# A 1408-column gate/up unit cut into three matmul pieces of 470, 470 and 468 columns in place of four of 352

## The chip, the cores and the metric

The program runs on one core of a Trainium2 chip, as one launch. The metric is device microseconds of that core for one execution; lower is better. Engines are named as in the profile: PE is TensorE (PEld its weight loads), DVE is VectorE, ACT is ScalarE, POOL is GpSimd, SP is SyncE, which starts the weight transfers. PSUM is the memory that TensorE writes: eight banks, each 512 float32 values wide in every one of 128 partitions.

## The reference: what is computed

Two decoder layers on 512 prompt tokens and 64 sample tokens, 576 rows of 1024 values. Each layer has three mixers (gated linear attention, a gated recurrence, dilated window attention), an output projection and a channel mixer. The channel mixer of layer 0 is a dense SwiGLU; that of layer 1, which the change touches, is a mixture of 8 experts of width 1408, two for each row:

```python
def swiglu(h, w_gate, w_up, w_down):
    return (jax.nn.silu(h @ w_gate) * (h @ w_up)) @ w_down

def moe_swiglu(h, w_router, w_gate, w_up, w_down):
    logits = (h @ w_router).astype(jnp.float32)
    top_v, top_i = lax.top_k(logits, TOP_K)
    gates = jax.nn.softmax(top_v, axis=-1)
    combine_w = jnp.sum(jax.nn.one_hot(top_i, N_EXPERTS, dtype=jnp.float32) * gates[..., None], axis=-2)
    out = jnp.zeros(h.shape, jnp.float32)
    for e in range(N_EXPERTS):
        out = out + combine_w[..., e:e + 1] * swiglu(h, w_gate[e], w_up[e], w_down[e]).astype(jnp.float32)
    return out.astype(h.dtype)
```

## The kernel before

**Items.** Rows are gathered by expert into items of 160 rows at most: 128 rows ("many") and 32 more ("few"). The count of items is data dependent; in the profiled run there are eight. Item 0 is written out (`item(None)`), the others run in a loop whose body is the same code. An expert's hidden width of 1408 is worked in two halves of `HID` = 704, and `CH` = 352 is half of that.

**Units.** Weights come in units of 128 input rows. A gate/up unit is 1408 columns wide: 704 columns of the gate, then the 704 of the up product for the same half. One half takes `KC` = 8 such units, since the model width is 8 x 128. A down unit is 1024 columns wide; a half has 6 or 5 of them. An item's order on TensorE, in `item`: 8 gate/up units of half 0, then 5 down units left over from the item before, then 8 gate/up units of half 1, then the 6 down units of half 0.

**Three passes.** Each float32 operand is split into a rounded part (hi) and the remainder (lo). ScalarE rounds a unit (L1087), VectorE takes the remainder (L2106), and `many_rows` (L1599 to L1606) multiplies every piece of the unit three times: hi by hi, hi by lo, lo by hi. The 128 rows stand still in the array and the weights stream past, so a piece of 352 columns is a matmul of 128x352. Three buffers (`NW` = 3) hold split units, so ScalarE starts on unit j + 3 once TensorE has finished unit j.

**Banks.** `gate_up` writes the unit's four pieces into banks 0 to 3 from column 0: the gate is in banks 0 and 1, the up product in banks 2 and 3. The 32 few rows use bank 4 (`few_rows`, L1608), with unsplit weights, after the units k = 1 and k = 5. Down units write banks 5 and 6.

**The end of a half.** When the eighth unit is done, ScalarE takes silu of the gate (`gates`, L1111 and L1112 for the many rows, L1113 for the few) and counts `silu_ready` (named gates_ready in the program) up by one after each. VectorE multiplies by the up product (`hidden`, L2113 and L2115 for the many rows, L2117 and L2118 for the few), and the last product counts `hid_ready`. Before its first product VectorE waits for the first silu, before its second for the second, before the third for the third. TensorE meanwhile runs two down units and then waits for `hid_ready` in `turn_hidden`, which transposes the hidden rows (L1633, L1636). In half 0 of item 0 there are no down units, so the wait comes at once.

What sets the order is the program text alone: each engine runs its own list in order, with semaphores between the lists.

Of the kernel before, what the change touches and what calls it, by code (L numbers as in the profile page):

```python
# [23 lines left out]
ALU = mybir.AluOpType  # L24
ACT = mybir.ActivationFunctionType
AX = mybir.AxisListType

P = 128
# [4 lines left out]
KC = D_MODEL // P  # L33
# [7 lines left out]
FE = 11  # L41
# [57 lines left out]

CH = FE * P // 4  # L100
HID = 2 * CH
TURNED = (range(0, HID // P), range(HID // P, FE))
U_FIRST = 2 * KC + len(TURNED[0])
U_BODY = 2 * KC + FE
# [101 lines left out]
def build(nc, d):  # L206

    ctx = ExitStack()
    with ctx:
# [6 lines left out]
        def tiles(ap, n):  # L216
            return ap.rearrange("p (n t) -> p n t", n=n)
# [27 lines left out]
        with ExitStack() as over:  # L245
# [4 lines left out]
            Xh, Xl = (tiles(over.enter_context(nc.sbuf_tensor(n, [P, KC * P], F32R)), KC) for n in ("item_in_hi", "item_in_lo"))  # L250

        V = tiles(sb("values", (TT + 1) * D_MODEL), TT + 1)
        LIN = sb("linear", N_LIN)
# [12 lines left out]
        def carve(base, *sizes):  # L266
            out, o = [], 0
            for s in sizes:
                out.append(base[:, o:o + s])
                o += s  # L270
            return out
# [66 lines left out]
        ht_few = tiles(qk_[:, 64 + 2 * FE * P:64 + 2 * FE * P + FE * CAP2], FE)  # L338
        FEW_AT = 2 * P
        hid_rows = [LIN[0:w, n * FE * P:(n + 1) * FE * P] for n, w in enumerate((P, CAP - P))]  # L340
        gate_a, gate_b, gate_few = carve(LIN[:, 2 * FE * P:2 * FE * P + 3 * CH], CH, CH, CH)

        X_tok = tiles(LIN[:, 0:(TT + 1) * D_MODEL], TT + 1)
        XT = [H_tok[:, st, :] for st in range(2)]
# [23 lines left out]
        ps = ctx.enter_context(nc.psum_tensor("ps", [P, 8, 512], F32))  # L368
# [4 lines left out]
        def split(ap):  # L373
# [49 lines left out]
        silu_ready, hid_ready, ht_ps, ht_hi, ht_ready = (sem(n) for n in (  # L423
            "gates_ready", "hidden_rows_ready", "hidden_in_psum", "hidden_rounded", "hidden_split"))
# [405 lines left out]
        def _(act):  # L830
# [23 lines left out]
            for L in range(DEPTH):  # L854
# [138 lines left out]
                for n in range(N_STEP + 3):  # L993
# [7 lines left out]
                    k = n - 2  # L1001
# [6 lines left out]
                    k = n - 3  # L1008
# [57 lines left out]
            for tt in range(TT + 1):  # L1066
                rows = P if tt < TT else NS
                act.wait_ge(xtok_ps, tt + 1)
                k = 2 + 2 * (tt % 3)
# [3 lines left out]
            for tt in range(TT + 1):  # L1073
                rows = P if tt < TT else NS
                act.wait_ge(htok_ps, tt + 1)
                k = 2 * (tt % 2)
# [31 lines left out]
            def gates(before, j):  # L1108

                act.wait_ge(unit_done, item_unit(before, j) + (UD_ITEMS + 1))  # L1110
                nc.scalar.activation(gate_a, ps[:, 0, 0:CH], ACT.Silu).then_inc(silu_ready, 1)  # L1111
                nc.scalar.activation(gate_b, ps[:, 1, 0:CH], ACT.Silu).then_inc(silu_ready, 1)  # L1112
                nc.scalar.activation(gate_few[0:DH], ps[0:DH, 4, 0:CH], ACT.Silu).then_inc(silu_ready, 1)  # L1113

            def copy_hidden(step, half):
# [41 lines left out]
        def _(pe):  # L1157
# [33 lines left out]
            for L in range(DEPTH):  # L1191
# [6 lines left out]
                for half in range(2):  # L1198
                    for u in range(4):
                        w = split_unit(ring_n, 2)  # L1200
                        ring_n += 1
                        for kk in range(2):
                            k = 2 * u + kk
# [61 lines left out]
                for ct in range(CT):  # L1265
# [53 lines left out]
                    o = ATS_AT[ct]  # L1319
# [76 lines left out]
                for n in range(N_STEP + 3):  # L1396
                    if n < N_STEP:
# [4 lines left out]
                        for c in range(0, w, 256):  # L1402
                            e = min(c + 256, w)
# [5 lines left out]
                    k = n - 3  # L1409
                    if 0 <= k < N_STEP:  # L1410
# [4 lines left out]
                        for kb in range(i + 1):  # L1415
                            for h in range(2):
                                o, f = slice(h * DH, h * DH + DH), 512 + (2 * hp + h) * DH
# [3 lines left out]
                    k = n - 2  # L1421
# [16 lines left out]
                for b in range(NB + 2):  # L1438
# [12 lines left out]
                    if b < NB:  # L1451
# [4 lines left out]
                        for a in range(2):  # L1456
                            for hp in range(4):
                                o = slice(32 * hp, 32 * hp + 32)
                                nc.tensor.matmul(ps[o, a, :], Qs[:, b, hp, :], kc[hp // 2][:, hp % 2, a * 512:a * 512 + 512], start=True, stop=True)
                        for hp in range(4):  # L1460
                            o = slice(32 * hp, 32 * hp + 32)
                            op = nc.tensor.matmul(ps[o, 2, 0:NS], Qs[:, b, hp, :], QK[:, 4 + hp, SEQ:T], start=True, stop=True)
                        op.then_inc(ssc_done, 1)
                    if 1 <= b <= NB:
# [6 lines left out]
                        for half in range(2):  # L1471
                            vc = tiles(piece_landed(pe, L, b - 1, 2 + half), 4)
                            for c in range(4):
                                for m in range(2):
                                    r, e = slice(64 * m, 64 * m + 64), slice(256 * m, 256 * m + 256)
                                    op = nc.tensor.matmul(out[r, e], pt[:, 4 * half + c, r], vc[:, c, e], start=(half, c) == (0, 0), stop=False)  # L1476
                            if half:
                                for m in range(2):
                                    r, e = slice(64 * m, 64 * m + 64), slice(256 * m, 256 * m + 256)
# [119 lines left out]
            def many_rows(before, j, x, outs, first, last):  # L1599

                pe.wait_ge(ew_split, item_unit(before, j) + 1)
                w = [t[:, j % NW, :] for t in (EWh, EWl)]
                for o, out in outs:
                    for n, (a, b) in enumerate(PASSES):
                        op = nc.tensor.matmul(out, x[a], w[b][:, o:o + out.shape[-1]], start=first and n == 0, stop=last and n == 2)  # L1605
                op.then_inc(unit_done, 1)  # L1606
# [7 lines left out]

            def gate_up(before, j0):
                for k in range(KC):
                    many_rows(before, j0 + k, [x[:, k, :] for x in (Xh, Xl)], [(c * CH, ps[:, c, 0:CH]) for c in range(4)], k == 0, k == KC - 1)
                    if k % 4 == 1:
                        for k2 in range(k - 1, k + 3):
                            few_rows(before, j0 + k2, x_few[:, k2, :], ps[:, 4, 0:CH], k2 == 0, k2 == KC - 1)  # L1620
# [63 lines left out]
        def _(dve):  # L1684
            v = nc.vector
# [34 lines left out]
            for L in range(DEPTH):  # L1720
# [138 lines left out]
                for ct in range(CT):  # L1859
# [6 lines left out]
                    o = ATS_AT[ct]  # L1866
# [51 lines left out]
                for n in range(N_STEP + 1):  # L1918
# [11 lines left out]
                    k = n - 1  # L1930
# [8 lines left out]
                for b in range(NB + 2):  # L1939
# [22 lines left out]
                    if b >= 2:  # L1962
                        dve.wait_ge(os_turned, NB * L + b - 1)
                        o = ps[:, 6 + b % 2, 0:P].rearrange("p (h q) -> p h q", h=4)
# [143 lines left out]
            def hidden(step, half):  # L2108

                o = half * HID  # L2110
                few = hid_rows[1]
                dve.wait_ge(silu_ready, step * 3 + 1)
                v.tensor_tensor(hid_rows[0][:, o:o + CH], ps[:, 2, 0:CH], gate_a, ALU.mult)  # L2113
                dve.wait_ge(silu_ready, step * 3 + 2)
                v.tensor_tensor(hid_rows[0][:, o + CH:o + HID], ps[:, 3, 0:CH], gate_b, ALU.mult)  # L2115
                dve.wait_ge(silu_ready, step * 3 + 3)
                v.tensor_tensor(few[:, o:o + CH], ps[64:96, 4, 0:CH], gate_few[0:32], ALU.mult)  # L2117
                v.tensor_tensor(few[:, o + CH:o + HID], ps[96:128, 4, 0:CH], gate_few[32:64], ALU.mult).then_inc(hid_ready, 1)  # L2118

# [135 lines left out]
```

## Time and profile before

| what | value |
|---|---|
| timed runs | 2201.57, 2205.87, 2208.22 us |
| their median | 2205.87 us |
| span of the profiled execution (first to last instruction) | 2200.3 us |
| mean granted TensorE clock over it | 0.965 |
| gate/up matmuls of the many rows | 3 x 512 of 128x352 |
| experts' stage in the span | about 1638 to 2185 us |

For the profiled execution the page gives no time beside its span of 2200.3 us; what stands before the first and behind the last instruction is not in it. Each row of a timeline gives a start and a duration. Matmuls overlap and their ends are modelled, so what a matmul costs the engine is read from start to start, not from its duration. A bracket at a row's end says how long the engine was idle before it and which instruction ended that wait.

### The profile page before, as it was taken

The numbers are of one execution on the slowest core, as the hardware profiler recorded it, in microseconds if no ns is written. First come the engines' busy times: TensorE is split into PE (matmuls) and PEld (weight loads), VectorE is DVE, ScalarE is ACT, GpSimd is POOL, SyncE is SP. The second block draws the span as 40 slices with busy tenths as digits, with TensorE's granted clock in tenths as the row PEclk, the third lists the DMA queues.
The fourth block names the chain that finished last, engine by engine and source line by source line (L and its number), as shares of the span: only waits on it lengthen the run. The fifth ranks groups of instructions, "written<-read, shape, count | busy, mean of one in ns | idle before, by whom it ended". The sixth has DMA issues, their size and how long they took to land. (4 is left out here: it accounts for less than half of the span.)

```text
span 2200.3 us, 36316 instructions
## 1 busy us (share of the span) xinstructions
PE 2020.9 (92%) x15091; PEld 1726.2 (78%) x15091; DVE 1011.8 (46%) x1365; ACT 870.0 (40%) x1208; POOL 273.7 (12%) x330
## 2 busy tenths in 40 slices
PE   7999787789999999999999788788978999999997
PEld 5999676546899999998899777546777777777775
DVE  3235655551333322323134564542126666676664
ACT  3356333420222212223247333521225565666664
POOL 2000643000100000002000552000040110111001
PEclk9999889999999999999999978999989999999998
DMA  4452103293375347421452201284335877787874
GB/s 176 158 186 78 71 1 133 81 403 113 115 286 173 123 178 257 152 76 45 153 192 85 106 1 58 118 356 155 109 137 209 285 269 278 273 287 259 285 286 119
DMA packets 78408, 375.46 MB, mean 171 GB/s; under 512 B 10160, under 2 KB 10576, under 8 KB 69424
## 3 DMA queue, kind: packets, MB, share of 16 engines
q1 hardware_dynamic: 70992, 354.47, 43.9%
q0 software_dynamic: 7296, 19.23, 3.0%
q8 instruction: 95, 1.56, 0.3%
q14 instruction: 25, 0.20, 0.0%
HBM read 357.21 MB, written 84.37 MB: 201 GB/s over the span
## 5 line engine op out<-in xcount | busy, mean ns | idle before, releaser
L2106 DVE TENSOR_TENSOR expert_weights_lo<-weight_ring,expert_weights_hi 128x1408 fp32r<-128x1408 f32 (+1 forms) x141 | 203.4, 1475 | 100.6 <-ACT expert_weights_hi L1087 100.1
L1087 ACT ACTIVATE expert_weights_hi<-weight_ring 128x1408 fp32r<-128x1408 f32 (+1 forms) x144 | 178.3, 1263 | 97.9 <-PE ps L1605 97.9
L1167 PE MATMUL ps<-ffn_in_hi,weights_hi 128*128 128x288 f32 x704 | 208.7, 296 | 5.8 <-DVE weights_lo L1983 3.3
L1167 PE MATMUL ps<-ffn_in_lo,weights_hi 128*128 128x288 f32 x704 | 207.7, 295 | 0.0
L1167 PE MATMUL ps<-ffn_in_hi,weights_lo 128*128 128x288 f32 x704 | 207.0, 294 | 0.0
L1167 PE MATMUL ps<-proj_in_hi,proj_weights_hi 128*128 128x288 f32 x608 | 183.5, 302 | 0.0
L1605 PE MATMUL ps<-expert_weights_hi,item_in_hi 128*128 128x352 f32 x512 | 172.1, 336 | 9.2 <-DVE expert_weights_lo L2106 5.6
L1167 PE MATMUL ps<-proj_in_lo,proj_weights_hi 128*128 128x288 f32 x608 | 179.3, 295 | 0.0
L1167 PE MATMUL ps<-proj_in_hi,proj_weights_lo 128*128 128x288 f32 x608 | 178.7, 294 | 0.0
L1605 PE MATMUL ps<-expert_weights_hi,item_in_lo 128*128 128x352 f32 x512 | 166.2, 325 | 0.0
L1605 PE MATMUL ps<-expert_weights_lo,item_in_hi 128*128 128x352 f32 x512 | 166.0, 324 | 0.0
L1183 PE MATMUL ps<-constants 128*128 128x128 f32 x1004 | 142.4, 295 | 21.0 <-DMA normed_or_mixed<-s_hgrn 16.8
L1183 PEld LDWEIGHTS ps<-constants 128*128 128x128 f32 x1004 | 130.0, 206 | 28.4 <-issue 18.9
L2106 DVE TENSOR_TENSOR expert_weights_lo<-residual,expert_weights_hi 128x1408 fp32r<-128x1408 f32 (+1 forms) x72 | 103.5, 1442 | 80.0 <-ACT expert_weights_hi L1087 80.0
L1167 PEld LDWEIGHTS ps<-ffn_in_hi,weights_hi 128*128 128x128 f32 x704 | 131.9, 187 | 6.4 <-DVE weights_lo L1983 3.8
L1167 PEld LDWEIGHTS ps<-ffn_in_hi,weights_lo 128*128 128x128 f32 x704 | 132.6, 188 | 0.0
L1167 PEld LDWEIGHTS ps<-ffn_in_lo,weights_hi 128*128 128x128 f32 x704 | 132.2, 188 | 0.0
L1983 DVE TENSOR_TENSOR weights_lo<-weight_ring,weights_hi 128x1024 fp32r<-128x1024 f32 (+1 forms) x60 | 79.7, 1332 | 112.8 <-ACT weights_hi L1037 112.8
L1087 ACT ACTIVATE expert_weights_hi<-residual 128x1408 fp32r<-128x1408 f32 (+1 forms) x72 | 88.9, 1235 | 102.9 <-PE ps L1605 102.9
L1161 PE MATMUL ps<-normed_or_mixed,weight_ring 128*128 128x288 f32 x512 | 126.4, 410 | 1.1 <-DVE normed_or_mixed L1967 1.1
L1605 PEld LDWEIGHTS ps<-expert_weights_hi,item_in_hi 128*128 128x128 f32 x512 | 97.5, 191 | 33.7 <-DVE expert_weights_lo L2106 20.1
L1161 PEld LDWEIGHTS ps<-normed_or_mixed,weight_ring 128*128 128x128 f32 x512 | 98.2, 192 | 28.7 <-DVE normed_or_mixed L1967 1.5
(342 smaller groups left out, 4296.6 us busy)
## 6 DMA issues: line engine op xcount, KB each, us to landing
weight_ring<-w_gu_moe SPq DMA_DIRECT2D x89, 704.0 KB, 6.4
ok_s<-kcache SPq DMA_DIRECT2D x16, 2032.0 KB, 10.3
ov_s<-vcache SPq DMA_DIRECT2D x16, 2032.0 KB, 9.3
weight_ring<-w_dn_moe SPq DMA_DIRECT2D x55, 512.0 KB, 5.8
residual<-w_gu_moe SPq DMA_DIRECT2D x39, 704.0 KB, 6.4
weight_ring<-w_gu SPq DMA_DIRECT2D x44, 512.0 KB, 3.6
scratch<-kcache SPq DMA_DIRECT2D x20, 1024.0 KB, 10.6
scratch<-vcache SPq DMA_DIRECT2D x20, 1024.0 KB, 12.2
```

What stands on the lines that cost most here:

```text
L1087: nc.scalar.activation(EWh[:, j % NW, 0:w], slot[:, 0:w], ACT.Copy).then_inc(ew_hi, 1)
L1161: op = nc.tensor.matmul(out_pair[:, a, :], w, rhs[:, a * HALF:a * HALF + HALF], start=k == 0, stop=k == kn - 1)
L1167: op = nc.tensor.matmul(out, x, y, start=k == 0 and n == 0, stop=k == kn - 1 and n == 2)
L1183: nc.tensor.matmul(ps[:, bank, col:col + P], const["ones"], const["ones"], start=True, stop=True, skip_group_check=True)
L1605: op = nc.tensor.matmul(out, x[a], w[b][:, o:o + out.shape[-1]], start=first and n == 0, stop=last and n == 2)
L1983: v.tensor_tensor(Wl[:, j % NSPLIT, 0:w], ring[:, n % R, 0:w], Wh[:, j % NSPLIT, 0:w], ALU.subtract).then_inc(w_split, 1)
L2106: v.tensor_tensor(EWl[:, j % NW, 0:w], slots[q][:, 0:w], EWh[:, j % NW, 0:w], ALU.subtract).then_inc(ew_split, 1)
```

## The change

A gate/up unit's 1408 columns are cut at 470 and 940 in place of 352, 704 and 1056. Three pieces lie in banks 0, 1 and 2. The gate then ends in the middle of the second piece: its columns 470 to 703 are in bank 1 at 0 to 233, and the first 236 columns of the up product follow them in the same bank, at 234 to 469. ScalarE's two silus are 470 and 234 columns wide, VectorE's two products 236 and 468. VectorE waits for both silus before its first product.

```diff
+CUTS = (0, 470, 940, 2 * HID)
...
-        gate_a, gate_b, gate_few = carve(LIN[:, 2 * FE * P:2 * FE * P + 3 * CH], CH, CH, CH)
+        gate_many, gate_few = carve(LIN[:, 2 * FE * P:2 * FE * P + 3 * CH], 2 * CH, CH)
...
                 act.wait_ge(unit_done, item_unit(before, j) + (UD_ITEMS + 1))
-                nc.scalar.activation(gate_a, ps[:, 0, 0:CH], ACT.Silu).then_inc(silu_ready, 1)
-                nc.scalar.activation(gate_b, ps[:, 1, 0:CH], ACT.Silu).then_inc(silu_ready, 1)
+                nc.scalar.activation(gate_many[:, 0:CUTS[1]], ps[:, 0, 0:CUTS[1]], ACT.Silu).then_inc(silu_ready, 1)
+                nc.scalar.activation(gate_many[:, CUTS[1]:HID], ps[:, 1, 0:HID - CUTS[1]], ACT.Silu).then_inc(silu_ready, 1)
                 nc.scalar.activation(gate_few[0:DH], ps[0:DH, 4, 0:CH], ACT.Silu).then_inc(silu_ready, 1)
...
-                    many_rows(before, j0 + k, [x[:, k, :] for x in (Xh, Xl)], [(c * CH, ps[:, c, 0:CH]) for c in range(4)], k == 0, k == KC - 1)
+                    many_rows(before, j0 + k, [x[:, k, :] for x in (Xh, Xl)], [(o, ps[:, c, 0:e - o]) for c, (o, e) in enumerate(zip(CUTS, CUTS[1:]))], k == 0, k == KC - 1)
...
-                dve.wait_ge(silu_ready, step * 3 + 1)
-                v.tensor_tensor(hid_rows[0][:, o:o + CH], ps[:, 2, 0:CH], gate_a, ALU.mult)
                 dve.wait_ge(silu_ready, step * 3 + 2)
-                v.tensor_tensor(hid_rows[0][:, o + CH:o + HID], ps[:, 3, 0:CH], gate_b, ALU.mult)
+                up1 = CUTS[2] - HID
+                v.tensor_tensor(hid_rows[0][:, o:o + up1], ps[:, 1, HID - CUTS[1]:CUTS[2] - CUTS[1]], gate_many[:, 0:up1], ALU.mult)
+                v.tensor_tensor(hid_rows[0][:, o + up1:o + HID], ps[:, 2, 0:2 * HID - CUTS[2]], gate_many[:, up1:HID], ALU.mult)
                 dve.wait_ge(silu_ready, step * 3 + 3)
```

One line is added near the top, so most line numbers are higher by one after the change; the products of `hidden` are then L2115, L2116, L2118 and L2119.

On TensorE, the second gate/up unit of item 0 stands so before (expert_weights are the unit's hi and lo parts, item_in the item's 128 rows):

```order
L1605 MATMUL ps<-expert_weights_hi,item_in_hi 128x352
L1605 MATMUL ps<-expert_weights_lo,item_in_hi 128x352
L1605 MATMUL ps<-expert_weights_hi,item_in_lo 128x352
L1605 MATMUL ps<-expert_weights_hi,item_in_hi 128x352
L1605 MATMUL ps<-expert_weights_lo,item_in_hi 128x352
L1605 MATMUL ps<-expert_weights_hi,item_in_lo 128x352
L1605 MATMUL ps<-expert_weights_hi,item_in_hi 128x352
L1605 MATMUL ps<-expert_weights_lo,item_in_hi 128x352
L1605 MATMUL ps<-expert_weights_hi,item_in_lo 128x352
L1605 MATMUL ps<-expert_weights_hi,item_in_hi 128x352
L1605 MATMUL ps<-expert_weights_lo,item_in_hi 128x352
L1605 MATMUL ps<-expert_weights_hi,item_in_lo 128x352
```

and so after the change:

```order
L1606 MATMUL ps<-expert_weights_hi,item_in_hi 128x470
L1606 MATMUL ps<-expert_weights_lo,item_in_hi 128x470
L1606 MATMUL ps<-expert_weights_hi,item_in_lo 128x470
L1606 MATMUL ps<-expert_weights_hi,item_in_hi 128x470
L1606 MATMUL ps<-expert_weights_lo,item_in_hi 128x470
L1606 MATMUL ps<-expert_weights_hi,item_in_lo 128x470
L1606 MATMUL ps<-expert_weights_hi,item_in_hi 128x468
L1606 MATMUL ps<-expert_weights_lo,item_in_hi 128x468
L1606 MATMUL ps<-expert_weights_hi,item_in_lo 128x468
```

Twelve matmuls became nine; nothing changed places with anything else, and all other units of item 0 and of the loop's body change in the same way.

On VectorE, at the end of half 0 of item 0 (linear holds the gates and the hidden rows), before:

```order
L2113 TENSOR_TENSOR linear<-ps,linear 128x352 [waits gates_ready]
L2115 TENSOR_TENSOR linear<-ps,linear 128x352 [waits gates_ready]
L2117 TENSOR_TENSOR linear<-ps,linear 32x352 [waits gates_ready]
L2118 TENSOR_TENSOR linear<-ps,linear 32x352
L2106 TENSOR_TENSOR expert_weights_lo<-weight_ring,expert_weights_hi 128x1408 [waits expert_unit_hi]
```

and after:

```order
L2115 TENSOR_TENSOR linear<-ps,linear 128x236 [waits gates_ready]
L2116 TENSOR_TENSOR linear<-ps,linear 128x468
L2118 TENSOR_TENSOR linear<-ps,linear 32x352 [waits gates_ready]
L2119 TENSOR_TENSOR linear<-ps,linear 32x352
L2107 TENSOR_TENSOR expert_weights_lo<-weight_ring,expert_weights_hi 128x1408 [waits expert_unit_hi]
```

Two products over 128 partitions are still two; the first is narrower, the second wider, and the wait between them now stands, with the later count, ahead of the first.

On ScalarE, at the same place, before:

```order
L1111 ACT_TABLE_LOAD
L1111 ACTIVATE linear<-ps 128x352 [waits unit_done]
L1112 ACTIVATE linear<-ps 128x352
L1113 ACTIVATE linear<-ps 64x352
L1087 ACTIVATE expert_weights_hi<-weight_ring 128x1408 [waits unit_done,expert_unit_in7]
```

and after:

```order
L1112 ACT_TABLE_LOAD
L1112 ACTIVATE linear<-ps 128x470 [waits unit_done]
L1113 ACTIVATE linear<-ps 128x234
L1114 ACTIVATE linear<-ps 64x352
L1088 ACTIVATE expert_weights_hi<-weight_ring 128x1408 [waits unit_done,expert_unit_in7]
```

The first silu is wider and the second narrower by as much; the order is the same.

## Rows read from the trace of the kernel before

**Rows 1.** The page: span, TensorE's busy line, the chain by line.

```profile
span 2200.3 us, 36316 instructions
PE 2020.9 (92%) x15091; PEld 1726.2 (78%) x15091; DVE 1011.8 (46%) x1365; ACT 870.0 (40%) x1208; POOL 273.7 (12%) x330
PE ps L1605 16%; PE ps L1612 5%; PE ps L1161 4%; DVE expert_weights_lo L2106 1%; ACT expert_weights_hi L1087 1%; POOL slot_table L780 1%; DMA scratch<-vcache 1%; PE ps L1633 1%; PE ps L1592 0%; PE ps L1636 0%; PE ps L1594 0%; PE ps L1476 0%; PE ps L1564 0%; DMA values<-normed_rows,attn_qk 0%; DMA slot_table<-attn_qk 0%
```

**Rows 2.** Busy by stretch; columns: stretch, length, busy (count) by engine, PEclk, DMA.

```profile
1638.00:1690.00 52.00, 46.72 (x327) 39.02 (x328) 25.48 (x22) 23.38 (x22) 2.92 (x8) 0.90 0.51 187
1757.00:1824.00 67.00, 66.22 (x513) 52.22 (x512) 45.70 (x41) 41.08 (x48) 8.43 (x10) 1.00 0.79 277
```

**Rows 3.** Waits of TensorE, 1638 to 2200; columns: us in total, times, longest.

```profile
PE ps L1605 <- DVE expert_weights_lo L2106: 6.0, 15, 0.5
PE ps L1633 <- DVE linear L2118: 3.4, 1, 3.4
```

**Rows 4.** Line L1605: ns min/median/max, first and last start, forms.

```profile
L1605 PE MATMUL ps<-expert_weights_hi,item_in_hi x512: 320/322/662, 1638.2 to 2160.7; 128*128 128x352 f32 x171
```

**Rows 5.** Timeline, TensorE, gate/up units; columns: start us, us, what.

```profile
1779.16 0.32 PE L1605 MATMUL ps<-expert_weights_hi,item_in_hi 128*128 128x352 f32 x1
1782.97 0.32 PE L1605 MATMUL ps<-expert_weights_hi,item_in_hi 128*128 128x352 f32 x1
...
1676.39 0.32 PE L1605 MATMUL ps<-expert_weights_lo,item_in_hi 128*128 128x352 f32 x1
1683.76 0.32 PE L1605 MATMUL ps<-expert_weights_hi,item_in_lo 128*128 128x352 f32 x1
```

**Rows 6.** Timeline, TensorE: 288 and 512 columns elsewhere, 512 in down units.

```profile
45.27 0.39 PE L1213 MATMUL ps<-proj_weights_hi,proj_in_hi 128*128 128x512 f32 x1
50.71 0.39 PE L1213 MATMUL ps<-proj_weights_hi,proj_in_hi 128*128 128x512 f32 x1
...
1099.79 0.29 PE L1167 MATMUL ps<-proj_in_hi,proj_weights_lo 128*128 128x288 f32 x1
1102.99 0.29 PE L1167 MATMUL ps<-proj_in_hi,proj_weights_lo 128*128 128x288 f32 x1
...
1798.35 0.39 PE L1605 MATMUL ps<-expert_weights_lo,hidden_turned_hi 128*128 128x512 f32 x1
1803.40 0.40 PE L1605 MATMUL ps<-expert_weights_hi,hidden_turned_lo 128*128 128x512 f32 x1
```

**Rows 7.** Timeline, TensorE, at the lower clock.

```profile
1667.90 0.49 PE L1605 MATMUL ps<-expert_weights_hi,item_in_lo 128*128 128x352 f32 x1
1669.95 0.49 PE L1605 MATMUL ps<-expert_weights_hi,item_in_hi 128*128 128x352 f32 x1
```

**Rows 8.** Timeline, all engines, where the gates are taken.

```profile
1824.80 0.32 PE L1605 MATMUL ps<-expert_weights_hi,item_in_lo 128*128 128x352 f32 x1
1825.16 0.46 ACT L1111 ACTIVATE linear<-ps 128x352 f32<-128x352 f32 x1 [0.84 <-PE ps L1605]
1825.52 0.46 ACT L1112 ACTIVATE linear<-ps 128x352 f32<-128x352 f32 x1
1825.65 0.52 DVE L2113 TENSOR_TENSOR linear<-ps,linear 128x352 f32<-128x352 f32 x1
1827.16 0.52 DVE L2118 TENSOR_TENSOR linear<-ps,linear 32x352 f32<-32x352 f32 x1
1827.48 0.39 PE L1605 MATMUL ps<-expert_weights_hi,hidden_turned_lo 128*128 128x512 f32 x1
1827.71 1.23 DVE L2106 TENSOR_TENSOR expert_weights_lo<-weight_ring,expert_weights_hi 128x1024 fp32r<-128x1024 f32 x1
...
1827.73 0.64 PEld L1633 LDWEIGHTS ps<-constants,linear 128*128 128x128 f32 x6 [0.29 <-DVE linear L2118]
...
1832.95 0.50 PE L1605 MATMUL ps<-expert_weights_hi,hidden_turned_hi 128*128 128x512 f32 x1
```

**Rows 9.** Line L2118: who waited for it; columns: us, times.

```profile
  PEld ps L1633: 8.0, 16
```

## The prediction, made before the changed kernel ran

> **What bounds the kernel now.** I read the page first: TensorE is busy for 92% of the span, and of the lines on the chain that ended last, L1605 has the largest share, 16% [rows 1]. L1605 is the line of the change. Next comes the table by stretch: in the experts' stage, over 67 us of one item, TensorE is busy for 66.22 us at a granted clock of 1.00, that is the 2.4 GHz level, while VectorE has 45.70 us and ScalarE 41.08 us [rows 2]. So the stage is TensorE's own stream, and a microsecond taken from it or put into it shows in the end. The waits say where the stream is broken. From 1638 us on, TensorE waits 15 times for a split unit (6.0 us in all), which is the start of a run of gate/up units after down units, and once for 3.4 us at L1633, the transposes of the hidden rows [rows 3]. That last row hides something: TensorE's weight loader waits at the same line for VectorE's last product L2118, 16 times out of 16 [rows 9]. So the end of each half is a tie between two engines, and the change touches both sides of it. These are the two terms: the cost of a gate/up unit, and the time of `hid_ready`.
>
> **Term 1: nine matmuls in place of twelve.** A half has 8 units, an item 2 halves, and there were 8 items: 128 units, 12 matmuls each, 1536 in all; the row has one pass of three, 512 [rows 4]. The columns stay 3 x 1408 = 4224 a unit, so a gain can only come from what a matmul costs beside its columns. I read that from start to start. Elsewhere in the program, two streams with the same kind of 128x128 weights run without a break: 24 steps of 512 columns take 50.71 - 45.27 = 5.44 us, 226.7 ns each; 24 steps of 288 columns take 1102.99 - 1099.79 = 3.20 us, 133.3 ns each [rows 6]. The line through both has 0.4167 ns a column (one column per cycle at 2.4 GHz) and 13.3 ns beside. For 352 it gives 160.0 ns. The units themselves: two units from 1779.16 to 1782.97 are 24 steps of 158.8 ns, and 46 steps from 1676.39 to 1683.76 are 160.2 ns [rows 5]. The line holds to 1%.
>
> So 470 columns should take 209.2 ns and 468 take 208.3: a unit is 6 x 209.2 + 3 x 208.3 = 1880 ns. Before it is 12 x 158.8 = 1905 or 12 x 160.2 = 1922. The gain is 25 to 42 ns a unit; I take 34. At the 1.2 GHz level it is nothing: 7 steps from 1667.90 to 1669.95 take 293 ns each, which is 352 columns at one per cycle with nothing beside [rows 7]. Some two or three units at the start of the stage run there, so 125 units count: 125 x 34 ns = 4.2 us less.
>
> The bounds. Above, 42 x 125 = 5.3 us. Below, the down units of the same stage take 229.5 ns for 512 columns (22 steps from 1798.35 to 1803.40), not 226.7 [rows 6]. If a wide matmul in this stage has that supplement, 470 lies between 160.2 at 352 and 229.5 at 512, at 211.3 ns, and a unit at 1899: 6 to 23 ns a unit, down to 0.8 us. I stay at 4.2, as the nearest rows, those of the same units, are on the clean line.
>
> Here a rule of the Trainium skill can be set against the rows. "TensorE: Matmul & The Clock Gate", section "Back-to-back issue gap", gives a step of N/2.4 + 2.5 ns. Three steps fewer would then be worth 7.5 ns a unit, an estimate of 1 us in all. The rows have 13.3 at two widths, so the measurement decides.
>
> **What hides behind a unit.** ScalarE and VectorE split units at widths that don't change, and TensorE's unit gets shorter by 2%. Within a run of gate/up units TensorE shows no wait before (24 steps of equal length across unit limits) [rows 5]. The first unit after down units still starts when its split is ready; that chain begins at a down unit and isn't touched, so those 6.0 us stay [rows 3].
>
> **Term 2: the hidden rows come later.** The timeline at the end of a half reads so [rows 8]. The unit's last matmul starts at 1824.80. ScalarE's first silu runs 1825.16 to 1825.62, the second 1825.52 to 1825.98. VectorE's first product starts at 1825.65, 0.03 us behind the first silu. Four products later L2118 ends at 1827.16 + 0.52 = 1827.68, and the transposes' weight load starts at 1827.73, 0.05 us after it. TensorE had its last down matmul at 1827.48 and would have gone on one 512 step later, at about 1827.71. The tie is won by VectorE by about 0.02 us.
>
> After the change VectorE's first product waits for both silus. The two silus have 704 columns in two instructions, as before, so the second ends as before at 1825.98 and the product starts at 1826.01: 0.36 us later. The two products have 704 columns in two instructions, as before, and the two of the few rows don't change; all four run back to back for the same 2.03 us. So `hid_ready` comes 0.36 us later, and as TensorE already waits for it, the whole of it is on TensorE. That happens 16 times: 16 x 0.36 = 5.8 us more.
>
> The bounds: four products of 0.52 us, the length of L2113 and L2118, would be 2.08 us end to end, and they take 2.03. If that overlap of 0.05 us is lost or doubled with the new widths, the delay is 0.41 or 0.31 us: 5.0 to 6.6 us in all. What is queued behind the waiting product on VectorE are the remainders of the next units: L2106 at 1827.71 goes to 1828.07. The down unit that follows the transposes starts at 1832.95, and moves with them [rows 8]; 3.6 us of cover stay. ScalarE's roundings behind the silus are not moved. DMA is at a share of 0.79 and sees the same units at the same pace [rows 2].
>
> **The sum.** -4.2 + 5.8 = +1.6 us. The profiled span is 2200.3 us, and the timed median 2205.87 stands 0.25% over it; the terms are microseconds of the same stage, so I add them to the median: 2207.5 us. By the bounds of this case alone it is -5.3 + 5.0 = -0.3 at best and -0.8 + 6.6 = +5.8 at worst, 2205.6 to 2211.7. A difference under 0.3%, 6.6 us, can't be told from no change by a measurement of this kernel.
>
> **Rivals.**
>
> *The gain without the wait.* The transposes don't come later, because TensorE's down units stretch or VectorE catches up. Then only term 1 is left: 2205.9 - 4.2 to - 5.3, about 2201. Against it stands the wait at 16 places of 16 [rows 9]: there is no slack on VectorE's side. For it, only that the tie is close. Chance 0.07. It too is under 6.6 us.
>
> *The new starts cost (slower).* Before, each piece of a unit starts at a multiple of 1408 bytes in the weights' row; after, two of the three start at 1880 and 3760 bytes. No row shows a stream from such a place. If TensorE reads those slower, the price falls on 6 matmuls of 9, 768 in all. From 6.6 ns a matmul, 3% of 209, it adds 5.1 us to the 1.6 and the kernel is slower than can be missed: at 5%, 10 ns, +9.6 us, 2215. For it: nothing but that the place is new. Against it: a unit's pieces start at four different places before, and their mean step is on the line [rows 5, 6]. Chance 0.08.
>
> *A matmul costs by the piece, not by the column (faster).* A unit would fall to 9/12 of 1.91 us, 0.48 us less, 60 us over 125 units: 2152 with term 2. The same section of the Trainium skill gives 131 ns for 512 columns and 81 for 128 as the sustained pace of load and matmul pairs, a far weaker growth with the width than one column per cycle; an estimate from it would be 24 us less. The rows have 133.3 ns at 288 and 226.7 at 512 [rows 6], so the chance is 0.01.
>
> **How the numbers follow.** The forecast has 0.84 (nearly all of it within 0.3%), the gain alone 0.07 (within 0.3%), new starts 0.08 (slower), cost by the piece 0.01 (faster). Scatter of the timed runs, 2201.57 to 2208.22, can push either way by a few microseconds, which I count as 0.03 more for each side. So faster 0.04, within 0.3% 0.85, slower 0.11. The range runs from the gain alone to just over the upper bound of the forecast: 2201 to 2212.5.
>
> **What would show it.** Term 1: steps of 209 ns at the 470 columns, 128 units of 1.88 us; 211 or more says that the supplement of the down units is in it, 216 or more the new starts. Term 2: VectorE's first product starting 0.03 us behind the second silu, and 0.6 us from the start of the last down matmul to the transposes' weight load, where it was 1827.73 - 1827.48 = 0.25. The weight loader's waits at that line grow from 8.0 us by 5.8. The forecast is wrong if the whole stage moves by more than 7 us, or if it gets shorter by over 1 us.

## The result and the profile after

The changed kernel is slower: 2211.73 us median against 2202.53 for the kernel before, 22 runs each, ratio 1.0036 with a 95% interval of 1.0026 to 1.0047. That is +7.9 us (5.7 to 10.4), by the mean times; the medians are 9.2 us apart. The time lies in the stated range and on the side of the forecast's sign, but the forecast was +1.6 us and "within 0.3%" had 0.85 of the chance; the ratio is just past that bound, and its interval reaches to both sides of it. That the time is in the range at all is in part luck. The range was built on a median of three runs, 2205.87 us, and 22 runs of the same kernel have 2202.53. The measured +7.9 put on 2205.87 would be 2213.8, over the range's end of 2212.5, and the worst sum of the forecast's own bounds was +5.8.

The page of the changed kernel, against [rows 1]:

```profile
span 2209.9 us, 35534 instructions
PE 2025.9 (92%) x14707; PEld 1698.1 (77%) x14707; DVE 1012.1 (46%) x1365; ACT 870.9 (39%) x1208; POOL 273.6 (12%) x330
PE ps L1606 14%; PE ps L1613 5%; PE ps L1162 4%; DVE expert_weights_lo L2107 1%; ACT expert_weights_hi L1088 1%; PE ps L1634 1%; POOL slot_table L781 1%; DMA scratch<-vcache 1%; PE ps L1593 0%; DVE linear L2119 0%; PE ps L1637 0%; DVE linear L2118 0%; PE ps L1595 0%; ACT linear L1113 0%; PE ps L1477 0%
```

The span is 9.6 us longer, TensorE has 384 matmuls fewer and is yet busy 5 us longer. Now the first term. The changed line's own count, and two unit starts of one run of gate/up units, columns as in [rows 5]:

```profile
L1606 PE MATMUL ps<-expert_weights_hi,item_in_hi x384: 367/376/762, 1640.0 to 2169.9; 128*128 128x470 f32 x128, 128*128 128x468 f32 x64
```

```profile
1954.35 0.38 PE L1606 MATMUL ps<-expert_weights_hi,item_in_hi 128*128 128x470 f32 x1
1958.18 0.38 PE L1606 MATMUL ps<-expert_weights_hi,item_in_hi 128*128 128x470 f32 x1
```

There are 3 x 384 = 1152 matmuls in place of 1536, as planned. From the first to the last start this line takes 2169.9 - 1640.0 = 529.9 us, where L1605 took 2160.7 - 1638.2 = 522.5 [rows 4]: in the two profiled executions the stage differs by 7.4 us, more than the 7 us that the prediction named as a sign that it is wrong. From 1954.35 to 1958.18 lie two units, 18 steps: 1.915 us a unit, 212.8 ns a step. Forecast were 1.880 us and 209 ns; before it was 1.905 to 1.922 [rows 5]. **Nothing was gained.** A table behind the experiments has more units.

The second term, on the timeline at the end of a half, all engines, against [rows 8]:

```profile
1966.42 0.38 PE L1606 MATMUL ps<-expert_weights_hi,item_in_lo 128*128 128x468 f32 x1
1966.83 0.57 ACT L1112 ACTIVATE linear<-ps 128x470 f32<-128x470 f32 x1 [0.85 <-PE ps L1606]
1967.29 0.36 ACT L1113 ACTIVATE linear<-ps 128x234 f32<-128x234 f32 x1
1967.68 0.40 DVE L2115 TENSOR_TENSOR linear<-ps,linear 128x236 f32<-128x236 f32 x1 [0.45 <-ACT linear L1113]
1968.00 0.63 DVE L2116 TENSOR_TENSOR linear<-ps,linear 128x468 f32<-128x468 f32 x1
1969.18 0.52 DVE L2119 TENSOR_TENSOR linear<-ps,linear 32x352 f32<-32x352 f32 x1
1969.14 0.39 PE L1606 MATMUL ps<-expert_weights_hi,hidden_turned_lo 128*128 128x512 f32 x1
...
1969.76 0.64 PEld L1634 LDWEIGHTS ps<-constants,linear 128*128 128x128 f32 x6 [0.65 <-DVE linear L2119]
```

The last unit's last matmul starts at 1966.42. The second silu ends at 1967.29 + 0.36 = 1967.65, and VectorE's first product starts 0.03 us later, where before it followed the first silu. The four products take 1967.68 to 1969.70, 2.02 us (2.03 before). TensorE's last down matmul starts at 1969.14 and the transposes' weight load at 1969.76: 0.62 us, before 0.25. The forecast's 0.6 us stands here line by line. The waits add it up, against [rows 3, 9]; first TensorE's, then who waited for L2119, in us and times:

```profile
PE ps L1634 <- DVE linear L2119: 7.2, 16, 3.8
PE ps L1606 <- DVE expert_weights_lo L2107: 5.8, 15, 0.5
...
  PEld ps L1634: 14.0, 16
```

Sixteen waits of the weight loader grew from 8.0 to 14.0 us, +6.0 (forecast +5.8), and TensorE's own wait at this place, seen once before, is now seen 16 times. The waits for split units are what they were, 5.8 us for 6.0.

One row of each trace gives the length of the whole stretch from the first silu to the last, 15 half items, before and after:

```profile
L1111 ACT ACTIVATE linear<-ps x16: 464/464/466, 1661.8 to 2161.4; 128x352 f32<-128x352 f32 x16
```

```profile
L1112 ACT ACTIVATE linear<-ps x16: 562/566/566, 1664.7 to 2170.7; 128x470 f32<-128x470 f32 x16
```

2161.4 - 1661.8 = 499.6 us before, 2170.7 - 1664.7 = 506.0 after: +6.4. Fifteen delays of 0.36 are 5.4; where most of the other 1.0 may come from stands in the account of the sum below.

### The profile page after: what moved, and what is told of

Same layout as the page of the kernel before. It is cut to its first block and busy times, and to the rows that moved or that the text cites. A ratio compares the mean times of both kernels' runs of the same rounds, so it can differ in the third digit from the quotient of the medians.

```text
span 2209.9 us, 35534 instructions
## 1 busy us (share of the span) xinstructions
PE 2025.9 (92%) x14707; PEld 1698.1 (77%) x14707; DVE 1012.1 (46%) x1365; ACT 870.9 (39%) x1208; POOL 273.6 (12%) x330
## 5 line engine op out<-in xcount | busy, mean ns | idle before, releaser
L1606 PE MATMUL ps<-expert_weights_hi,item_in_hi 128*128 128x470 f32 (+1 forms) x384 | 151.7, 395 | 9.1 <-DVE expert_weights_lo L2107 5.4
L1606 PE MATMUL ps<-expert_weights_lo,item_in_hi 128*128 128x470 f32 (+1 forms) x384 | 146.3, 381 | 0.0
L1606 PE MATMUL ps<-expert_weights_hi,item_in_lo 128*128 128x470 f32 (+1 forms) x384 | 145.8, 380 | 0.0
L1725 DVE TENSOR_TENSOR proj_weights_lo<-weight_ring,proj_weights_hi 128x1024 fp32r<-128x1024 f32 x54 | 70.2, 1299 | 106.5 <-ACT proj_weights_hi L869 106.5
```

Source lines behind the costliest of these rows:

```text
L1725: v.tensor_tensor(Ul[:, u % 2, :], ring[:, (RING0[L] + u) % R, 0:1024], Uh[:, u % 2, :], ALU.subtract).then_inc(u_split, 1)
```

## The experiments

**late_product: term 2 alone.** Four pieces of 352 as before, with the later wait.

```diff
-                dve.wait_ge(silu_ready, step * 3 + 1)
+                dve.wait_ge(silu_ready, step * 3 + 2)
                 v.tensor_tensor(hid_rows[0][:, o:o + CH], ps[:, 2, 0:CH], gate_a, ALU.mult)
-                dve.wait_ge(silu_ready, step * 3 + 2)
```

> The kernel before, four pieces of 352, with one thing of the change alone: VectorE waits for both silus ahead of its first product. Theory 1 (the later product alone makes the loss): the transposes start 0.36 us later in each of 16 halves, 5.8 us, ratio 1.0026, and gate/up units stay at 1.907 to 1.920 us from start to start. Rival (the loss is in the wide matmuls, the tie is absorbed): ratio 1.000 and no growth of the wait at the transposes.

Measured: 1.0017 (1.0003 to 1.0031). In its trace, VectorE's first product at the end of a half, and the weight loader's waits for the last product (us, times, longest):

```profile
1968.61 0.53 DVE L2113 TENSOR_TENSOR linear<-ps,linear 128x352 f32<-128x352 f32 x1 [0.47 <-ACT linear L1112]
...
PEld ps L1633 <- DVE linear L2117: 13.7, 16, 4.1
```

The product waits 0.47 us for the second silu, and the weight loader's waits are 13.7 us against 8.0 before [rows 9]. One edit in the waits gives the second term by itself, 5.7 us in the trace; the ratio's interval, 0.7 to 6.8 us, holds it, with 3.7 us in its middle.

**even_cuts, four_uneven: do the starts matter?** First the changed kernel with pieces of 512, 448 and 448.

```diff
-CUTS = (0, 470, 940, 2 * HID)
+CUTS = (0, 512, 960, 2 * HID)
```

> The changed kernel with cuts at 512 and 960 (pieces of 512, 448 and 448) in place of 470 and 940, so that every piece starts and ends at a multiple of 64 columns; the wait for both silus stays. Theory 1 (the odd starts and widths cost the 4 ns that a wide matmul takes over the line): a unit falls from 1.916 to 1.880 us, 128 units give back 4 to 5 us, ratio to before 1.0005 to 1.001. Rival (a wide matmul in this stage costs its supplement whatever the cut): a unit stays at 1.91 to 1.92 us, ratio to before about 1.003.

Measured: 1.0024 (1.0011 to 1.0037). Two unit starts on TensorE's timeline:

```profile
1950.78 0.40 PE L1606 MATMUL ps<-expert_weights_hi,item_in_hi 128*128 128x512 f32 x1
1954.59 0.40 PE L1606 MATMUL ps<-expert_weights_hi,item_in_hi 128*128 128x512 f32 x1
```

1.905 us a unit: 0.01 under the changed kernel, not 0.036. The ratio lies between what the two theories asked for; its interval holds the rival's 1.003 and leaves out theory 1's 1.0005 to 1.001. Then the kernel before with uneven pieces (the silus and VectorE's products are cut at 350 columns too):

```diff
-... [(c * CH, ps[:, c, 0:CH]) for c in range(4)] ...
+... [(c * CH - c % 2 * 2, ps[:, c, 0:CH + c % 2 * 4 - 2]) for c in range(4)] ...
```

> The kernel before with four pieces of 350, 354, 350 and 354 columns in place of four of 352; waits as before. Theory 1 (odd starts and widths cost): 12 matmuls of a unit each take 3 to 5 ns more, a unit goes from 1.907 to 1.920 up to 1.945 to 1.975, +4 to +7 us over 128 units, ratio 1.002 to 1.003. Rival (width alone, or the stage, sets the supplement): units stay within 0.01 us, ratio 1.000.

Measured: 1.0003 (0.9989 to 1.0017). Two unit starts:

```profile
1944.98 0.32 PE L1605 MATMUL ps<-expert_weights_hi,item_in_hi 128*128 128x350 f32 x1
1948.84 0.32 PE L1605 MATMUL ps<-expert_weights_hi,item_in_hi 128*128 128x350 f32 x1
```

1.93 us a unit, 0.01 to 0.025 over the kernel before: under theory 1's 1.945, and over the 0.01 us of the rival. So uneven pieces may cost something, 25 ns a unit at the most, but late_product, with even pieces of 352, has units up to 1.934 us too, and even_cuts changed the widths along with the starts. No run shows such a cost by itself, and it is not the missing 34 ns.

**five_pieces: is there a cost per matmul at all?**

```diff
-CUTS = (0, 470, 940, 2 * HID)
+CUTS = (0, 512, 1024, 2 * HID)
+PIECES = ((0, 0, 0, 256), (256, 0, 256, 256), (512, 1, 0, 256), (768, 1, 256, 256), (1024, 2, 0, 384))
...
-... [(o, ps[:, c, 0:e - o]) for c, (o, e) in enumerate(zip(CUTS, CUTS[1:]))], k == 0, k == KC - 1)
+... [(o, ps[:, c, at:at + n]) for o, c, at, n in PIECES], k == 0, k == KC - 1, (256, 768))
```

The last argument names the pieces that lie second in a bank; their first matmul adds to what is there, since the piece ahead of them has started the bank.

> The changed kernel with five pieces of 256, 256, 256, 256 and 384 columns (two share bank 0, two share bank 1): 15 matmuls a unit. Theory 4 (a matmul costs its columns and 13.3 ns, and only the wide ones of this stage carry a supplement): steps of 120 ns at 256 and 173 at 384, a unit 1.96 us. Rival (this stage takes a unit's columns at one pace however they are cut): a unit at 1.91 to 1.92 us as with 12 and with 9 matmuls.

Measured once, with a profile: 2220.85 us, where the kernel before, run once beside it, has 2198.66. A unit's start, the start of its piece of 384 columns, and the next unit but one:

```profile
1960.81 0.28 PE L1607 MATMUL ps<-expert_weights_hi,item_in_hi 128*128 128x256 f32 x1
...
1962.23 0.34 PE L1607 MATMUL ps<-expert_weights_hi,item_in_hi 128*128 128x384 f32 x1
...
1964.71 0.28 PE L1607 MATMUL ps<-expert_weights_hi,item_in_hi 128*128 128x256 f32 x1
```

1.95 us a unit with 15 matmuls: a cost per matmul is there. By the table below it is some 6 ns each for the six more than in the changed kernel, and 14 ns each for the three more than before. Twelve steps of 256 columns from 1960.81 to 1962.23 are 118 ns each, near the line of [rows 6] with 120. The wide ones are off it: 384 columns take 174 to 178 where the line has 173.3. Of the 22 us by which this one run is longer, the units explain some 5 and the weight loader's longer waits, 13.5 us for 8.0, as much again; the rest is not explained.

The units of the runs so far, read at more places: the fourth and the fifth unit of both halves of items 1 to 7, 28 in each trace, from the start of the unit's first matmul to the start of the next unit's.

| kernel | pieces of a unit | mean unit, us | shortest, longest |
|---|---|---|---|
| before | 4 x 352 | 1.911 | 1.906, 1.920 |
| late_product | 4 x 352 | 1.920 | 1.906, 1.934 |
| four_uneven | 350, 354, 350, 354 | 1.933 | 1.933, 1.934 |
| changed | 470, 470, 468 | 1.918 | 1.915, 1.921 |
| even_cuts | 512, 448, 448 | 1.906 | 1.892, 1.914 |
| five_pieces | 4 x 256, 384 | 1.953 | 1.953, 1.954 |

The two kernels with the same matmuls, before and late_product, differ by 9 ns; the changed kernel lies between them.

**moved_tiles, pass_outer, one_stationary, one_moving, idle_split: what makes the wide ones slow?** Each changes one thing in the changed kernel. The tiles' places:

```diff
-            EWh, EWl = ...
             Xh, Xl = ...
+            EWh, EWl = ...
```

> The changed kernel (470, 470, 468) with the tiles of the item's rows (item_in_hi, item_in_lo) placed ahead of the split weights in place of behind them, so that the weight loads and the streamed operand read other addresses; nothing else. Theory 2 (a weight load that reads beside a stream costs the stream some ns, by where the two lie): the pattern of steps by position changes and a unit leaves 1.916 us by more than 10 ns, either way. Rival (width alone): the same steps at the same positions, a unit at 1.91 to 1.92.

```profile
1954.48 0.38 PE L1606 MATMUL ps<-expert_weights_hi,item_in_hi 128*128 128x470 f32 x1
1958.32 0.38 PE L1606 MATMUL ps<-expert_weights_hi,item_in_hi 128*128 128x470 f32 x1
```

The passes' order:

```diff
-                for o, out in outs:
-                    for n, (a, b) in enumerate(PASSES):
+                for n, (a, b) in enumerate(PASSES):
+                    for o, out in outs:
```

> The changed kernel with the three passes outside and the three pieces inside, so that successive matmuls write different banks and have the same weights in the array three times. Theory 3 (adding into the same bank three times running costs a wide matmul its supplement): steps of 470 columns fall from 213 to 209 ns, a unit to 1.88 us. Rival (width or addresses): a unit within 10 ns of 1.916 us.

```profile
1955.87 0.80 PE L1606 MATMUL ps<-expert_weights_hi,item_in_hi 128*128 128x470 f32 x3
1959.71 0.80 PE L1606 MATMUL ps<-expert_weights_hi,item_in_hi 128*128 128x470 f32 x3
```

The weights in the array (row starts of the second matmul of a unit):

```diff
-... [x[:, k, :] for x in (Xh, Xl)] ...
+... [x[:, k, :] for x in (Xh, Xh)] ...
```

> The changed kernel with the rounded rows standing in the array in all three passes (the remainder of the item's rows is left out of the gate and up products). Theory 2 (weight loads reading beside the stream): the steps ahead of and behind the third pass change, a unit leaves 1.916 us by more than 5 ns. Rival (width alone): the same steps.

```profile
1954.90 0.37 PE L1606 MATMUL ps<-expert_weights_lo,item_in_hi 128*128 128x470 f32 x1
1958.74 0.38 PE L1606 MATMUL ps<-expert_weights_lo,item_in_hi 128*128 128x470 f32 x1
```

The streamed tile:

```diff
-                        op = nc.tensor.matmul(out, x[a], w[b][:, o:o + out.shape[-1]], ...
+                        op = nc.tensor.matmul(out, x[a], w[0 if out.shape[-1] < 500 else b][:, o:o + out.shape[-1]], ...
```

> The changed kernel with the rounded weights streamed in all three passes of the gate and up products (the weights' remainder is left out of them): the streamed address no longer alternates between the two tiles. Theory 2b (the alternation between tiles costs wide matmuls their supplement): steps of 470 columns at 209 ns, a unit at 1.88 us. Rival (width in this stage): a unit within 10 ns of 1.916 us.

```profile
1951.89 0.59 PE L1606 MATMUL ps<-expert_weights_hi,item_in_hi 128*128 128x470 f32 x2
1955.73 0.59 PE L1606 MATMUL ps<-expert_weights_hi,item_in_hi 128*128 128x470 f32 x2
```

ScalarE and VectorE beside the stream (the first row is a table by stretch: length, busy of PE, PEld, DVE, ACT, POOL, then PEclk and DMA's share):

```diff
-                nc.scalar.activation(EWh[:, j % NW, 0:w], slot[:, 0:w], ACT.Copy).then_inc(ew_hi, 1)
+                c = w if before is None and j < NW else 16
+                nc.scalar.activation(EWh[:, j % NW, 0:c], slot[:, 0:c], ACT.Copy).then_inc(ew_hi, 1)
...
-                v.tensor_tensor(EWl[:, j % NW, 0:w], slots[q][:, 0:w], EWh[:, j % NW, 0:w], ALU.subtract).then_inc(ew_split, 1)
+                v.tensor_tensor(EWl[:, j % NW, 0:16], slots[q][:, 0:16], EWh[:, j % NW, 0:16], ALU.subtract).then_inc(ew_split, 1)
```

> The changed kernel with ScalarE's rounding and VectorE's remainder cut to 16 of a unit's columns (from the fourth unit on; the other columns stay as an earlier unit left them), so that both engines are nearly idle beside TensorE. Theory 5 (their traffic in SBUF slows the wide streams): steps of 470 columns at 209 ns, a unit at 1.88 us. Rival (TensorE alone sets it): a unit at 1.91 to 1.92 us; only the waits at the start of a run of units, 6 us in all, go. Both: the transposes still come 3.3 us after the last unit's last matmul.

```profile
1890.00:1957.00 67.00, 66.54 (x470) 49.20 (x468) 11.77 (x42) 14.39 (x50) 6.66 (x10) 1.00 0.79 278
...
1939.38 0.38 PE L1607 MATMUL ps<-expert_weights_hi,item_in_hi 128*128 128x470 f32 x1
1943.22 0.38 PE L1607 MATMUL ps<-expert_weights_hi,item_in_hi 128*128 128x470 f32 x1
```

Two units take 3.84 us in all five, 1.92 us each, the rival's figure every time. In the last one VectorE is busy for 11.77 us of 67 where it had 45.70 [rows 2], and ScalarE for 14.39 in place of 41.08, and the unit is the same. Of the five times, one run each, 2212.11, 2213.64, 2212.06, 2209.17 and 2192.36 us, only the last moves. With it TensorE's waits for split units go, 5.8 us in the changed kernel; its first gate/up matmul also starts at 1633.6 us of the span, 4 to 10 us sooner than in the other four, which is ahead of anything that the edit touches. So no one of these by itself makes wide matmuls slow here: not the places tried, nor the banks' order, nor the alternation of either operand, nor most of the two other engines' work. None of the five changes the weight transfers; DMA's share is 0.79 in the row above, as it is before [rows 2]. What slows the wide matmuls stays open.

**early_even, few_between: three pieces without the later product.** The pieces are those of even_cuts, 512, 448 and 448. ScalarE takes the short silu first; VectorE starts with the 192 columns that need it alone.

```diff
+                nc.scalar.activation(gate_many[:, CUTS[1]:HID], ps[:, 1, 0:HID - CUTS[1]], ACT.Silu).then_inc(silu_ready, 1)
                 nc.scalar.activation(gate_many[:, 0:CUTS[1]], ps[:, 0, 0:CUTS[1]], ACT.Silu).then_inc(silu_ready, 1)
-                nc.scalar.activation(gate_many[:, CUTS[1]:HID], ps[:, 1, 0:HID - CUTS[1]], ACT.Silu).then_inc(silu_ready, 1)
...
+                dve.wait_ge(silu_ready, step * 3 + 1)
+                v.tensor_tensor(hid_rows[0][:, o + 2 * n:o + HID], ps[:, 2, n:2 * HID - CUTS[2]], gate_many[:, 2 * n:HID], ALU.mult)
                 dve.wait_ge(silu_ready, step * 3 + 2)
...
+                up = tiles(ps_flat[:, at:at + 2 * (1024 - at)], 2)[:, :, 0:n]
+                v.tensor_tensor(tiles(hid_rows[0][:, o:o + 2 * n], 2), up, tiles(gate_many[:, 0:2 * n], 2), ALU.mult)
```

Here n is 256, half of the first piece, and `at` is the column where the up product starts when banks are counted as one row.

> Pieces of 512, 448 and 448 with ScalarE's short silu (192 columns of bank 1) ahead of the long one (512 of bank 0), VectorE's first product 192 columns wide behind the first silu, and its second 512 wide, over parts of banks 1 and 2, behind the second. Both terms then point the same way. Theory 1: units at 1.880 us save 4 to 5 us, the hidden rows come at the time of before within 0.05 us, ratio 0.9975 to 0.9985. Rival (wide matmuls cost their supplement whatever the cut): units at 1.91 to 1.92, ratio 1.000.

Measured: 1.0006 (0.9993 to 1.0019). The second kernel puts the few rows' silu and products between the two of the many rows:

```diff
+                nc.scalar.activation(gate_few[0:DH], ps[0:DH, 4, 0:CH], ACT.Silu).then_inc(silu_ready, 1)
                 nc.scalar.activation(gate_many[:, 0:CUTS[1]], ps[:, 0, 0:CUTS[1]], ACT.Silu).then_inc(silu_ready, 1)
-                nc.scalar.activation(gate_few[0:DH], ps[0:DH, 4, 0:CH], ACT.Silu).then_inc(silu_ready, 1)
...
```

VectorE's products follow in the same order, each behind its own silu.

> The kernel early_even (pieces 512, 448, 448, the short silu first) with the few rows' silu ahead of the long one, and VectorE's order: 192 columns, the two products of the few rows, then the 512 columns. VectorE then runs its four products without a break from the end of the short silu: the hidden rows about 0.1 us sooner than in early_even, the transposes 2.95 to 2.99 us after the last unit's last matmul in place of 3.07. Theory 1 (the tie decides, units cost what they cost): 16 halves x 0.1 us = 1.6 us under early_even, ratio to the kernel before 0.9985 to 1.0005. Rival (TensorE's own down units end no sooner): ratio as early_even, 1.0006.

Measured: 1.0005 (0.9989 to 1.0021). The weight loader's waits for VectorE's last product, first in early_even, then in few_between:

```profile
PEld ps L1636 <- DVE linear L2123: 9.8, 16, 3.9
```

```profile
PEld ps L1636 <- DVE linear L2123: 7.9, 16, 3.8
```

9.8 and then 7.9 us, where the changed kernel has 14.0 and the kernel before 8.0 [rows 9]. In early_even the hidden rows are so about 0.11 us later than before in each half, not within the 0.05 that was expected, and few_between takes that back; the times of the two can't be told apart. With the second term gone three pieces neither gain nor cost what these runs can tell. No kernel that does the whole of the work beats the one before.

## Why the prediction was right in one term and wrong in the other

- **What bounds the kernel** held: the stage is TensorE's stream, and the tie at the end of each half was real. A wait of 0.36 us, put ahead of VectorE's first product, showed in the weight loader's waits 16 times, with 0.375 us in the mean.
- **Term 2** was right in mechanism and size: +5.8 forecast, +6.0 in the changed kernel's waits, +5.7 with the wait changed alone. The product starts 0.03 us behind the second silu and the four products keep their 2.03 us, as worked out.
- **Term 1 failed**, at the sentence "So 470 columns should take 209.2 ns". The line through 288 and 512 columns was read from other parts of the program, and in the experts' stage it doesn't hold for wide pieces: 352 columns have 159 to 160 ns (line 160.0), but 384 have 174 to 178 (173.3), 470 have 213 (209.2) and 512, in even_cuts, 232 (226.7). Twelve times 160 and nine times 213 are both 1.92 us. The lower bound named the right rows, the stage's own down units at 229.5 ns for 512 columns, but its straight line from 352 to there gave 211.3 ns for 470 and a gain of at least 6 ns a unit; I stayed with the clean line because the 352 columns were on it. The measured gain is nil, outside the bounds of the term. The mean steps of all the widths that were run in this stage, 256 to 512, also lie within 1.3 ns of another straight line, 0.442 ns a column and 5.0 ns a matmul. By that line there is no width at which a supplement sets in; a column costs more here and a matmul less than was read elsewhere. The runs don't tell the two readings apart.
- **The rule of the Trainium skill** that was weighed (page "TensorE: Matmul & The Clock Gate", section "Back-to-back issue gap", N/2.4 + 2.5 ns, which the section gives for an isolated matmul) came nearer the gain of nil, an estimate of 1 us, by no merit of its own: 470 columns would be 198 ns by it, and 213 were measured.
- **The rivals.** "The new starts cost" needed 6.6 ns on each of six matmuls, 40 ns a unit; at most some 10 to 25 ns can be in it, and no run shows even that apart from the widths and from the scatter between kernels. "A matmul costs by the piece" is refuted once more by the 15 matmuls a unit that take 1.95 us. "The gain without the wait" fell with both of its halves: the wait came, and early_even and few_between, with most or all of it taken back, showed no gain.
- **The sum** is then 0 + 5.8, at the lower end of the measured 5.7 to 10.4 us. Some 2 us of the 7.9 stay open, and the interval allows that they are nothing. For the two profiled executions a part of it can be read: TensorE's clock in item 0. The rows have two stretches, each before and after, PEclk being the third figure from the end; then the second stretch and the row of the first silu in moved_tiles.

```profile
1638.00:1646.00 8.00, 7.78 (x56) 6.38 (x56) 2.33 (x3) 2.77 (x2) 2.92 (x8) 0.76 0.34 91
...
1664.00:1680.00 16.00, 14.04 (x90) 11.98 (x91) 6.23 (x7) 5.29 (x7) 0.00 (x0) 0.79 0.28 98
```

```profile
1638.00:1646.00 8.00, 5.99 (x16) 5.13 (x16) 1.85 (x3) 2.74 (x4) 2.73 (x7) 0.50 0.27 82
...
1664.00:1680.00 16.00, 10.73 (x60) 7.88 (x60) 7.77 (x10) 6.85 (x10) 0.00 (x0) 0.68 0.22 85
```

```profile
1664.00:1680.00 16.00, 10.58 (x62) 7.69 (x64) 8.13 (x10) 8.12 (x11) 0.00 (x0) 0.79 0.29 106
...
L1112 ACT ACTIVATE linear<-ps x16: 563/563/563, 1666.0 to 2170.8; 128x470 f32<-128x470 f32 x16
```

The changed kernel's stream stayed at 1.2 GHz (0.50) until past 1646 us in this execution, with its start 1.8 us later; the kernel before rose within the stretch. Behind TensorE's longest wait of the stage, 3.4 us before and 3.8 after, the clock is low again, and again for longer in the changed kernel: a mean of 0.68 over 16 us in place of 0.79, made of 0.50 and 1.00, is 10.2 us at the lower level in place of 6.7. moved_tiles has the changed kernel's instructions and 0.79 here, and from its first silu to its last are 2170.8 - 1666.0 = 504.8 us, 5.2 over the kernel before, where the changed kernel has 6.4. So about 1 us of the profiled difference goes with the clock of item 0. Other kernels with wide pieces show both courses, so it may be chance, and no run here settles how often it comes in the timed runs.
- **What can be measured** was put too low: the prediction said that a difference under 6.6 us can't be told from no change, and 22 runs of each kernel give an interval 4.7 us wide.

## What to carry to other kernels

A cost per instruction read in one stage is not a price in another: before fewer, wider matmuls are counted as a gain, run the wide one in the same stream; here even a line between two widths of the same stage was 2 ns short. When two engines tie at a hand-over, a regrouping that makes the later engine wait for a second piece can be paid in full, as it was at all 16 places here, so look first at which result the first consumer needs and produce that one first.

## What the runs showed of the hardware that was not expected

Full-width streams of one kernel keep two paces at the same granted clock of 1.00. The down units of the kernel before show both behind one another, at the very end, where DMA's share is 0.01 (the second figure from the end of the first row, a stretch of 11 us); then three starts from TensorE's timeline:

```profile
2175.00:2186.00 11.00, 10.57 (x81) 7.11 (x79) 5.55 (x5) 3.51 (x4) 0.00 (x0) 1.00 0.01 1
...
2180.13 0.40 PE L1605 MATMUL ps<-expert_weights_lo,hidden_turned_hi 128*128 128x512 f32 x1
2182.23 0.39 PE L1605 MATMUL ps<-expert_weights_lo,hidden_turned_hi 128*128 128x512 f32 x1
2183.82 0.39 PE L1605 MATMUL ps<-expert_weights_hi,hidden_turned_lo 128*128 128x512 f32 x1
```

From 2180.13 to 2182.23 lie 9 steps of 233 ns, from 2182.23 to 2183.82 lie 7 of 227. So the slower pace of these down units needs no transfer beside them. In the projections 512 columns keep 226.7 over 24 steps [rows 6]; none of the 28 gate/up units of 512 and 448 columns in even_cuts came down to the line, which has 1.880 us for them (1.892 to 1.914). A stream's pace of about 2.2 columns a nanosecond (4224 in 1.92 us) came back with 9 matmuls a unit in the changed kernel and in all five variants of it. Its cause was not found.
